# Modulation weights with features on partitions, row sums on VectorE, gates through DRAM

## The reference

```
cs = silu(c)                                  # 2048
mod = cs @ w_ada + b_ada                      # 2048 x 12288
sh1, sc1, gt1, sh2, sc2, gt2 = split(mod, 6)  # 2048 each
h = rmsnorm(x, g_pre_mix) * (1 + sc1) + sh1
y = attention branches and projections of h
x = x + gt1 * rmsnorm(y, g_post_mix)
h = rmsnorm(x, g_pre_ffn) * (1 + sc2) + sh2
f = square(relu(h @ w_ff1)) @ w_ff2
x = x + gt2 * rmsnorm(f, g_post_ffn)
```

## Time and profile before

| | before |
|---|---|
| median of three runs | 1755.67 us |
| span of the profiled execution (its own time is shown by its span alone) | 1753.4 us |
| TensorE busy | 1741.4 us, 8058 matmuls |
| VectorE busy | 1274.5 us, 1665 instructions |
| ScalarE busy | 871.8 us |
| GpSimd busy | 240.8 us |
| DMA moved | 461 MB, 263 GB/s on average |
| mean granted TensorE clock | 0.999 |

### The profile page before, as it was taken

How to read it: one execution, slowest core, us unless ns; L and a number is a source line. 1 busy time by engine, 2 the same in 40 slices (tenths; PEclk the granted TensorE clock), 3 DMA queues, 4 the chain that set the end, 5 groups by cost and what they waited for, 6 DMA issues and landing times.

```text
span 1753.4 us, 24782 instructions
## 1 busy us (share of the span) xinstructions
PE 1741.4 (99%) x8058; PEld 1437.4 (82%) x8058; DVE 1274.5 (73%) x1665; ACT 871.8 (50%) x1205; POOL 240.8 (14%) x451
## 2 busy tenths in 40 slices
PE   9999999999999999999999999999999999999998
PEld 7877778887888888888888888888888888888886
DVE  5898879768988788777679778777765654445555
ACT  7866674544534444544445455444444444444443
POOL 1332401101144233300001100000000000000000
PEclk9999999999999999999999999999999999999999
DMA  9999869464789888898989848999987775555553
GB/s 350 311 340 326 299 253 382 144 199 156 258 256 294 290 269 282 288 306 296 318 302 317 313 150 284 329 313 316 311 277 240 227 228 192 192 192 194 193 193 138
DMA packets 145424, 461.12 MB, mean 263 GB/s; under 512 B 21728, under 2 KB 33744, under 8 KB 144720
## 3 DMA queue, kind: packets, MB, share of 16 engines
q1 hardware_dynamic: 109200, 344.46, 58.5%
q0 software_dynamic: 36016, 115.83, 19.7%
q10 hardware_dynamic: 144, 0.03, 0.0%
HBM read 436.13 MB, written 12.06 MB: 256 GB/s over the span
## 4 chain that ended last, share of the span: by engine, by line
PE 98%; DVE 1%; ACT 1%; DMA 0%; SPq 0%; issue 0%; DVEq 0%; ACTq 0%
PE bank L1781 31%; PE bank L1782 31%; PE bank L1783 31%; PE bank L1827 1%; PE bank L2073 0%; PE bank L2086 0%; DVE x L1174 0%; PE bank L1952 0%; PE bank L1807 0%; DMA raw<-in_w_in_a 0%; ACT y L700 0%; PE bank L1943 0%; PE bank L1941 0%; DVE y L1773 0%; PE bank L2087 0%; PE bank L2072 0%
## 5 line engine op out<-in xcount | busy, mean ns | idle before, releaser
L1145 DVE TENSOR_TENSOR w_lo<-raw,w_hi 128x1024 fp32r<-128x1024 f32 x605 | 731.5, 1214 | 407.9 <-ACT w_hi L696 406.4
L696 ACT ACTIVATE w_hi<-raw 128x1024 fp32r<-128x1024 f32 x605 | 634.1, 1050 | 738.8 <-PE bank L1783 636.2
L1781 PE MATMUL bank<-w_hi,h_hi 128*128 128x512 f32 x2272 | 890.5, 392 | 2.1 <-DVE w_lo L1257 1.8
L1783 PE MATMUL bank<-w_hi,h_lo 128*128 128x512 f32 x2272 | 885.0, 390 | 0.0
L1782 PE MATMUL bank<-w_lo,h_hi 128*128 128x512 f32 x2272 | 885.0, 390 | 0.0
L1781 PEld LDWEIGHTS bank<-w_hi,h_hi 128*128 128x128 f32 x2272 | 426.6, 188 | 95.8 <-issue 7.9
L1783 PEld LDWEIGHTS bank<-w_hi,h_lo 128*128 128x128 f32 x2272 | 426.6, 188 | 89.0
L1782 PEld LDWEIGHTS bank<-w_lo,h_hi 128*128 128x128 f32 x2272 | 426.7, 188 | 86.7
L559 POOL DMA_DIRECT2D ada_raw<-in_w_ada x160 | 85.5, 534 | 693.8 <-DVE acc_a L1152 505.1
L1152 DVE SCALAR_TENSOR_TENSOR acc_a<-ada_raw,cond,acc_a 128x1024 f32<-128x1024 f32 x112 | 142.8, 1278 | 10.4 <-DMA ada_raw<-in_w_ada 10.4
L1152 DVE SCALAR_TENSOR_TENSOR acc_b<-ada_raw,cond,acc_b 128x1024 f32<-128x1024 f32 x48 | 61.3, 1279 | 11.8 <-DMA ada_raw<-in_w_ada 11.8
(11 more groups left out here) (243 smaller groups left out, 929.4 us busy)
## 6 DMA issues: line engine op xcount, KB each, us to landing
raw<-in_w_ff SPq DMA_DIRECT2D x256, 512.0 KB, 4.6
raw<-in_w_in SPq DMA_DIRECT2D x176, 512.0 KB, 5.0
ada_raw<-in_w_ada POOLq DMA_DIRECT2D x160, 512.0 KB, 6.6
raw<-in_w_in_a SPq DMA_DIRECT2D x69, 512.0 KB, 5.9
ada_more<-in_w_ada POOLq DMA_DIRECT2D x32, 512.0 KB, 6.8
raw<-in_w_out_a SPq DMA_DIRECT2D x32, 512.0 KB, 5.9
raw<-in_w_o SPq DMA_DIRECT2D x32, 512.0 KB, 4.9
raw<-in_w_moba SPq DMA_DIRECT2D x16, 512.0 KB, 6.4
```

Of the source, the lines that this page charges most:

```text
L696: act.activation(used(w_hi, turn, s), used(raw, turn, s), ACT.Copy).then_inc(hi_ready, 1)
L1145: dve.tensor_tensor(used(w_lo, turn, s), used(raw, turn, s), used(w_hi, turn, s).bitcast(F32), ALU.subtract).then_inc(lo_ready, 1)
L1781: pe.matmul(out_ap, hi, rhs_hi, start=start, stop=False)
L1783: return pe.matmul(out_ap, lo, rhs_hi, start=False, stop=stop)
```

## The change

The weights are laid out in DRAM with the output feature on partitions: a tile is 128 output features by 1024 features of `c`, one contiguous piece, and there are still 192. The condition is a row of 2048 in all partitions: `c` is spread by one DMA of 1 MB on POOL's queue ahead of the first tiles, and ScalarE applies Silu to it in slot 2 of TURN_Q (before, the small condition was made in the first turn). VectorE makes product and row sum of a tile in one instruction, into one column of `mod_part` (or of `loop_sums` in loops, copied at the end of a pass by `keep_sums`). The first four tiles are used in slots 3, 5, 6 and 7 of TURN_Q. The sums of two half tiles, the bias and the gain are added in six small steps for each scale and shift (`make_mod`, slot 1 of the residual turn) and five for each gate (`make_gate`). `mod_sums`, `rows`, `round_gate`, `gate_gain`, `read_mod`, `read_rest`, the clearing and the bias loads go. A gate's column is turned in 32x32 blocks, written to DRAM by four DMAs and read back as a row in all partitions (`write_gate`, `load_gate_row`); the gains' own rows are no longer loaded. `ones_r` and the wait of TensorE on `gain_ready` go. The diff, cut to its core:

```diff
-    w_ad = w_ada.rearrange("(k p) n -> p k n", p=P)
+    w_ad = w_ada.rearrange("u p n -> p u n")
...
             def load_ada(m, slot, part, k, half, slots=2, first=False):
                 if not first:
                     pool.wait_ge(ada_done, m - slots + 1)
-                col = part * D + half * (D // 2)
-                pool.dma_start(two(ada_slot(slot), 1), w_ad[:, bass.ds(k, 1), col:col + D // 2])\
+                pool.dma_start(two(ada_slot(slot), 1), w_ad[:, bass.ds((k + part * KT) * 2 + half, 1), :])\
                     .then_inc(ada_loaded[slot], 16)
...
+            def write_gate(n):
+                home = gate_home[n, :].rearrange("(k q i) -> q k i", q=QUADS, i=QUAD)
+                pool.wait_ge(gate_col_turned, n + 1)
+                for q in range(QUADS):
+                    pool.dma_start(home[q], gate_t[q * QUAD:q * QUAD + KT, :]).then_inc(gate_written, 16)
+            def load_gate_row(n):
+                pool.wait_ge(gate_written, (n + 1) * QUADS * 16)
+                load_gain(n + 1, gate_home[n, :])
...
-            clear_acc(acc_a)
-            clear_acc(acc_b)
+            pool.memset(gate_col[:, :], 0.0).then_inc(gate_zero, 1)
             pool.wait_ge(xt_loaded[SLOTS + 1], 16)
             pool.dma_start(sink[:, :], sinks.partition_broadcast(P)).then_inc(sink_loaded, 16)
-            start_acc(acc_a, SC1, 0)
-            start_acc(acc_b, SH1, 1)
             pool.wait_ge(x_loaded[CHUNKS - 1], 16)
+            pool.dma_start(cond[:, :], c_in.partition_broadcast(P)).then_inc(cond_loaded, 16)
...
-            pool.wait_ge(mod_ready, 2)
-            init_acc(acc_a, GT1, 2)
-            init_acc(acc_b, SH2, 3)
+            pool.dma_start(mods[:, :], mods_in).then_inc(mods_loaded, 16)
...
                 if s == 2:
+                    act.wait_ge(cond_loaded, 16)
+                    act.activation(cond[:, :], cond[:, :], ACT.Silu).then_inc(cond_ready, 1)
                     load_sqrt()
                     norm_root()
-                if s == 3:
-                    act.wait_ge(ident_loaded, 16)
-                    act.activation(ones_r[:, :], ones, ACT.Copy).then_inc(ones_ready, 1)
...
-            def add_ada(m, slot, acc, k, half, loads):
+            def add_ada(slot, half, loads, dst):
                 dve.wait_ge(ada_loaded[slot], loads)
-                if not isinstance(m, int) or m > 1:
-                    dve.wait_ge(ada_done, m - 1)
-                part = acc[:, half * (D // 2):(half + 1) * (D // 2)]
-                dve.scalar_tensor_tensor(part, ada_slot(slot), cond[:, bass.ds(k, 1)], part, ALU.mult, ALU.add)\
-                    .then_inc(ada_done, 1)
+                w = ada_slot(slot)
+                dve.tensor_tensor_reduce(w, w, cond[:, half * (D // 2):(half + 1) * (D // 2)], 1.0, 0.0, ALU.mult, ALU.add,
+                                         dst).then_inc(ada_done, 1)
...
+            def keep_sums(done, part, k, first, count):
+                dve.wait_ge(ada_done, done)
+                dve.tensor_copy(mod_part[:, bass.ds(k + part * KT, count), :], loop_sums[:, first:first + count, :])\
+                    .then_inc(sums_kept, 1)
...
-                if s % 2:
-                    ada_first(0, s // 2, acc_a, s // 4)
+                if s == ADA_Q[0]:
+                    dve.wait_ge(cond_ready, 1)
+                if s in ADA_Q:
+                    n = ADA_Q.index(s)
+                    ada_first(0, n, mod_column(SC1, n // 2, n % 2))
...
+                    if s == 1:
+                        make_mod(r)
...
-                read_mod(r)
+                dve.wait_ge(mod_ready, r)
                 norm_first(r, pre_gain)
...
-                if s >= 4:
-                    gate_gain(0, s - 4, SCORES + s % 2)
+                if s == 4:
+                    make_gate(0)
...
-                    if s == TILE_FROM - 1:
-                        pe.wait_ge(ada_done, MOD_UNITS[r])
-                        pe.wait_ge(evicted[PAIR_B if r == 1 else PAIR_A][1], (6, 23)[r - 1])
-                        mod_sums(mod_bank(r), range(MOD_IN_TURN))
...
-                mod_sums(mod_bank(r), MOD_IN_GAPS[0])
                 for s in range(ahead):
                     norm_turned(r, s)
-                mod_sums(mod_bank(r), MOD_IN_GAPS[1]).then_inc(mod_columns, 1)
...
-                if 3 <= s <= 6:
-                    gate_sums(0, s - 3)
...
-                if s % 2:
-                    gate_sums(1, s // 2)
```

More of the change, by code:

```diff
@@ L24 @@
 EPS = 1e-6
-PAD_OPERANDS = 224
+PAD_OPERANDS = 20
 PAD_O = 56
@@ L360, in two_block_kernel @@
         TILE_FROM = UPT - SLOTS
-        MOD_IN_TURN = 3
-        MOD_IN_GAPS = (range(3, 15), range(15, 22), range(22, 2 * KT))
-        MOD_READ = 6
-        def mod_bank(r):
-            return pair[PAIR_B if r == 1 else PAIR_A][1]
-        rest_bank = pair[PAIR_B][1]
-        def gate_quarter(q):
-            return acc_a[:, q * CH:(q + 1) * CH]
         X_STATS = (0, 3, 10)
@@ L670, in _ @@
                 load_shift(n)
+            for n in (6, 7):
+                load_shift(n)
+            write_gate(0)
             pool.wait_ge(p2_moved, 4 * MOVES)
-            load_gain(1, g_post_mix)
-            for q in range(CHUNKS):
-                rest_of_sum(SUMS_GATE[0] + q, gate_quarter(q))
-                if q < 2:
-                    load_shift(6 + q)
-            pool.wait_ge(gain_ready, 4)
-            init_acc(acc_a, SC2, 4)
+            load_gate_row(0)
             with pool.Fori(0, CHUNKS - 1) as c:
@@ new lines, in summed, with make_mod @@
+            def summed(dst, part, step, first):
+                cols = slice(part * KT, (part + 1) * KT)
+                dve.tensor_tensor(dst, mod_part[:, cols, 0], mod_part[:, cols, 1], ALU.add).then_inc(step, 1)
+                dve.wait_ge(step, first + 1)
+                return dve.tensor_tensor(dst, dst, mods[:, cols], ALU.add)
+            def make_mod(r):
+                gain = (V_MIX, V_FFN)[r - 1]
+                dve.wait_ge(mods_loaded, 16)
+                dve.wait_ge(ada_done, MOD_UNITS[r - 1])
+                n = 3 * (r - 1)
+                summed(pre_gain[:, :], (SC1, SC2)[r - 1], mod_step, n).then_inc(mod_step, 1)
+                dve.wait_ge(mod_step, n + 2)
+                dve.scalar_tensor_tensor(pre_gain[:, :], pre_gain[:, :], 1.0, vecs[:, gain:gain + KT], ALU.add, ALU.mult)
+                summed(pre_shift[:, :], (SH1, SH2)[r - 1], mod_step, n + 2).then_inc(mod_ready, 1)
@@ new lines, in make_gate @@
+            def make_gate(n):
+                post = (M_POST_MIX, M_POST_FFN)[n]
+                gate = gate_col[:, 0:KT]
+                dve.wait_ge(gate_zero, 1)
+                dve.wait_ge(ada_done, GATE_UNITS[n])
+                summed(gate, (GT1, GT2)[n], gate_step, 3 * n).then_inc(gate_step, 1)
+                dve.wait_ge(gate_step, 3 * n + 2)
+                dve.tensor_tensor(gate, gate, mods[:, post:post + KT], ALU.mult).then_inc(gate_step, 1)
+                dve.wait_ge(gate_step, 3 * n + 3)
+                if n:
+                    dve.wait_ge(gate_written, n * QUADS * 16)
+                dve.transpose(gate_t[:, :], gate_col[:, :]).then_inc(gate_col_turned, 1)
@@ L1324, in _ @@
             first_turn(TURN_KV)
-            dve.wait_ge(cond_ready, 1)
-            for n in range(2):
-                dve.wait_ge(acc_init[n], 16)
             dve.wait_ge(sink_loaded, 16)
@@ L1721, in _, with ff1_turn @@
             square(PAIR_A, 23, 0)
-            dve.wait_ge(acc_init[5], 16)
-            def ff1_turn(c, units=0, m=0, n0=0, k0=0):
+            def ff1_turn(c, m, columns):
                 for s in range(UPT):
                     split(c + 1 + TURN_FF1, s + AHEAD)
-                    if s in ADA_FF1[0:units]:
-                        n = n0 + ADA_FF1.index(s)
-                        ada(m, n, acc_a, k0 + n // 2)
+                    if s in ADA_FF1[0:len(columns)]:
+                        n = ADA_FF1.index(s)
+                        ada(m, *columns[n])
             with dve.Fori(0, 5) as it:
                 for b in range(2):
-                    ff1_turn(it * 2 + b, 3, it * 6 + 160, 3 * b, it * 3)
+                    ff1_turn(it * 2 + b, it * 6 + 160, [(3 * b + n, loop_column(3 * b + n)) for n in range(3)])
                     square(1 - b, it + 25 - b, it * 2 + b + 1)
+                keep_sums(it * 6 + 166, GT2, it * 3, 0, 3)
+                dve.wait_ge(sums_kept, it + 16)
             for c in range(10, 14):
-                ff1_turn(c, 2 if c == 10 else 0, 190, 0, 15)
+                ff1_turn(c, 190, [(n, mod_column(GT2, 15, n)) for n in range(2)] if c == 10 else [])
+                if c == 11:
+                    make_gate(1)
                 square(1 - c % 2, c // 2 + 25 - c % 2, c + 1)
@@ L1803, in chunk_unit @@
                 unit(turn, s, h_hi, h_lo, KG * s, p, use, s == 0, s == UPT - 1, cols)
-            def mod_sums(bank, columns):
-                for c in columns:
-                    acc, k = (acc_a, acc_b)[c // KT], c % KT
```

(2 more changed lines are left out.)

220 lines of the change are left out of this document (74 added, 146 removed).

## The result

The changed kernel takes 1759.49 us (median of 20 runs, 1757.30 to 1762.80), the kernel before 1755.61 (20 runs, 1754.82 to 1756.86): ratio 1.0023 [1.0016, 1.0030], 3.9 us slower. 1753.3 was forecast, with a range up to 1756.5. The profiled execution took 1762.7 us (span 1761.0), one of the slowest of its runs.

What follows compares the result with a forecast made beforehand. TensorE's own work was taken to set the end (busy 1741.4 of 1753.4 us). 5.9 us removed, less 3.0 at the start and 0.5 in two attention passes, gave 2.4 us less: median 1753.3, range 1749.6 to 1756.5 us.

Steps and rivals of the forecast that it cites:

- What TensorE loses: Matmuls removed from TensorE at gates, residual turns and gaps: 5.9 us less, of 5.0 to 6.5.
- gates: Eight pairs of 128x512 gate-row matmuls go, each holding the next product back 0.46 us: 3.7 us less.
- columns in the turns: Three column sums in the middle of each residual turn go: 0.66 us, twice, 1.3 us less.
- The columns in the gaps: 29 columns per turn behind the residual turns, mostly filling idle time: 0.7 us gained in the first gap, 0.2 in the second.
- VectorE's step: 192 multiply-adds of 1.28 us become products with row sum: 0.06 us more per step, covered except in the first attention.
- the two passes: Second and third pass of the first attention: six dearer VectorE steps each stall TensorE 0.25 us, 0.5 us in all.
- Rival B: New VectorE step costs 2.4 us, not 1.28: 1771 us or more; chance 0.08 together with a start over 9 us.
- Gate rows through DRAM: Four small writes and a 1 MB row read back replace a 1 MB row, needed turns later: costs nothing.
- The start: Condition row, Silu and later tiles make VectorE's first scores late: TensorE loses 3.0 us, bounds nothing to 4.5.
- Rival A: Tile loads land sooner or VectorE catches up, so first scores stay within 1.2 us of lead: 1750.5 us; chance 0.34.
- C: Removed gap work was only filling, so only 3.7 + 1.3 us remain gained: 1754.2 us; chance 0.52 together with the forecast.
- The signs: Forecast wrong if TensorE waits after 205 us, the step exceeds 1.6 us, or ScalarE awaits the condition's row beyond 41 us.

Runs made afterwards that it cites:

- early_row: Changed kernel with the condition's row spread on the chip in place of the 1 MB load, first tiles used in their old slots: 1757.38 us, ratio 1.0009.
- before_start3: Kernel before plus a 1 MB row load, ScalarE's pass over it, and first four tiles used in slots 3, 5, 6, 7: 1760.26 us, ratio 1.0026.
- fill_first: `early_all` with only the first 12 and 7 idle products in each gap, without the last ten: 1751.68 us, one run.
- early_all: `early_row` with PAD_O 24 in place of 56 and idle 128x128 products in both gaps: 1750.62 us, ratio 0.9971.

## Why the prediction was wrong

- **What TensorE loses: right.** Forecast 3.7 + 1.3 + 0.9 = 5.9; measured 1.90 + 1.92 (gates), 2 x 0.72 (columns in the turns), 0.53 + 0.01 (gaps): 5.80.
- **What it costs to leave the gaps empty: not seen.** The columns in the gaps were priced only as work that may delay the chain (0.7 and 0.2 us); the clock had no term in the sum. They also kept TensorE's clock at its upper level. Without them it idles twice for over 2 us in each gap and starts on the lower one: 1.59 + 1.58 us in this execution, 2.40 + 1.72 in `early_row`'s. Taking work out from beside a wait was forecast to give 0.9 us; it gave 0.5 and cost 3.2.
- **Placement: not seen.** The diff showed `PAD_OPERANDS` going from 224 to 20, which keeps `raw` and the weights where they were, and left `PAD_O`; behind them 32 elements came in. 2.4 us. The prediction had no step for addresses, though the kernel has two pads.
- **VectorE's step: small as said, off in sign.** 0.06 us more per step was taken, and 0.5 us for the two passes; it takes 0.06 us less, and the passes cost 0.15. Rival B didn't come: 1219 ns for 1024 columns from two sources in SBUF with the row sum, beside 1278 without it. (Its sum was off too: six steps 1.12 us dearer are 6.7 us in a pass, not 6.4.)

  The Trainium skill's rule beside it ("Vector Engine (DVE) Microarchitecture Reference", "Points that are easy to get wrong", half the throughput) isn't seen in either of these rows. Whether the row sum, which the profile names CUSTOM_DVE_ANT_0, has the form that the rule names, no run here shows.
- **Gate rows through DRAM: nothing, as said.** TensorE waits for neither.
- **The start: the mechanism was right, the size too small.** Forecast 3.0 us between 60 and 205 us, with nothing ahead of it but 0.1; it is 7.5 in the profiled execution and some 4.1 in the median (3.88 more in all, plus 5.80, less 3.17 and 2.38), beside the 4.5 of `before_start3`. The step that failed is "ScalarE comes to it at 40.37 ... no wait ... Stall: 0.1 us". The row landed in time, but ScalarE came to it at 43.31, held by weights that landed late beside the row, and TensorE had lost 1.5 us to them by 38 us, ahead of Silu. Silu's 1.9 us came on top, with nothing between ScalarE and the keys that could take it up: 2.66 us were lost by 47 us. The medians give the pass 2.7 us over the bytes alone. The first tile was then used at 48.95, not 46.2, and the loads landed later as well: the fifth tile was issued at 61.7 and used 6.8 us later, where 5.6 was taken for its landing. And the wait of 3.4 us came with slow products behind it, as the gaps did.
- **Rival A (start covered)** didn't come, and nor did its landing of 3.2 us, an estimate from the Trainium skill's page "DMA: Bandwidth & Descriptors", section "Anatomy of one DMA — SWDGE (gpsimd) path": the tiles land after 6.4 us in the median. **C** had the gaps nearly right (0.5, not nothing, where the forecast had 0.9), but its 1754.2 is 5.3 us under the measured time, for the same reasons as the forecast.
- **The signs.** Of the three that would show the forecast wrong, one came: TensorE waits after 205 us, 4.8 us in each gap. The first units behind the gaps began 0.5 and 0.01 us sooner than before, near what was said, and then ran slow. The step took well under 1.6 us, and ScalarE never waited for the condition's row.

Of the error of 6.2 us, 3.2 is the clock in the gaps, 2.4 the placement, and 0.6 the start with the passes (4.1 in place of 3.5), with 0.1 for the removed work. The clock's part goes by one execution's gaps and was 4.1 in `early_row`'s, and the start's is what is left over, so each of these two is good to about 1 us. That the start looks nearly right in the median is in part luck: the forecast put its loss behind 60 us, and in the profiled execution a third of it arose before 47.

## What to carry to other kernels

Before taking work off the engine that sets the end, ask what that engine does in its place: if it idles ahead of a dense stretch, look at the granted clock there, and try a few idle products right ahead of it (here ten in each gap gave back what 29 did). After any change of the memory layout compare the distance between products turn by turn; a shift of 64 or 128 bytes per partition cost 2.4 us or more here and shows in no wait. And a pass put on a helper engine in a stretch without slack can cost its full length (some 2 to 3 us here for 1.9), although ScalarE is busy for only half of the span.

## What was unexpected of the hardware

- Products of 128x512 whose moving operand lies 16 or 32 elements further stand 0.2333 and 0.2324 us apart in place of 0.2267, in all four turns and in every trace with that layout.
- After idle stretches of 2.1 to 2.5 us, TensorE made some 6 to 12 products at 0.43 us each before it came back to 0.23; how many differs from one execution to the next. Not every such stretch does it: `fill_first` had the low clock behind one of its gaps and not behind the other, both after 2.3 us, and the scores in `before_start3` ran at full clock after 2.63 us (0.49 us for the group).
- VectorE's 32x32-block transpose takes a broadcast operand, and so spreads 64 values per partition into a row in all partitions: 0.70 us for 512 columns, four times, in place of 1 MB through the queues (`early_all`):

```profile
26.63 0.70 DVE L1264 STREAM_TRANSPOSE cond<-p_back 128x512 f32<-128x512 f32 x1
```
